# The last block's queries, keys, convolution input and gates: from TensorE transposes to VectorE blocks and a trip through DRAM

## The reference, cut to what matters

```
def hybrid_mixer(h, w_in, b_merge, conv_w, w_out_conv, w_out_attn, w_o):
    B, S, _ = h.shape
    proj = jnp.einsum("bsd,dc->bsc", h, w_in)
    splits = np.cumsum([D_CONV] * 4 + [D_ATTN] * 4 + [D_MODEL])
    xc, bg, cg, zc, q, k, v, za, g_conv, g_attn = jnp.split(proj, splits, axis=-1)

    c = causal_depthwise_conv(cg * xc, conv_w)
    y_conv = jnp.einsum("bsc,cd->bsd", jax.nn.silu(zc) * bg * c, w_out_conv)

    shp = (B, S, N_HEADS, HEAD_DIM)
    o = mixture_of_dilations(q.reshape(shp), k.reshape(shp), v.reshape(shp),
                             alibi_slopes(N_HEADS)).reshape(B, S, D_ATTN)
    y_attn = jnp.einsum("bsc,cd->bsd", jax.nn.silu(za) * o, w_out_attn)
    ...
    merged = g_conv * y_conv + g_attn * y_attn
    return jnp.einsum("bsd,de->bse", merged, w_o)
```

## Time and profile before

| | us |
|---|---|
| median of 3 runs | 1367.21 |
| lowest, highest | 1365.07, 1367.71 |
| the profiled execution, its own time | 1366.17 |
| its span in the profile | 1364.4 |
| PE busy, of the span | 1348.8 |
| VectorE, ScalarE, GpSimd busy | 624.0, 658.0, 1140.3 |

### The profile page before, as it was taken

One profiled execution on the slowest core, in us unless ns is written; L12 is line 12 of the kernel. 1 busy time (PEld: TensorE's weight loads), 2 busy tenths in 40 slices (PEclk: granted clock), 3 DMA queues, 4 the chain that ended last, 5 costly groups with the idle time before them and its releaser, 6 DMA issues.

```text
span 1364.4 us, 19630 instructions
## 1 busy us (share of the span) xinstructions
PE 1348.8 (99%) x6723; PEld 1121.2 (82%) x6723; DVE 624.0 (46%) x1570; ACT 658.0 (48%) x757; POOL 1140.3 (84%) x913
## 2 busy tenths in 40 slices
PE   8999999999999999999999999999999999999997
PEld 6888888888888888888888778888888888878886
DVE  6233344654333356623333885333346236862224
ACT  6444454546444456444443676444446443444431
POOL 5999977849999969999998539999978977779882
PEclk9999999999999999999999999999999999999999
DMA  8666654536666555766558426665545557767540
GB/s 273 215 201 208 206 183 144 185 106 225 197 192 194 194 171 171 237 210 211 184 184 217 139 77 208 210 198 187 184 154 196 192 193 202 215 183 256 190 165 31
DMA packets 199488, 255.36 MB, mean 187 GB/s; under 512 B 42844, under 2 KB 137860, under 8 KB 199300
## 3 DMA queue, kind: packets, MB, share of 16 engines
q1 hardware_dynamic: 197140, 247.82, 57.0%
q10 hardware_dynamic: 2288, 6.75, 1.4%
HBM read 249.29 MB, written 5.24 MB: 187 GB/s over the span
## 4 chain that ended last, share of the span: by engine, by line
PE 92%; DVE 4%; ACT 1%; DMA 1%; issue 1%; SPq 0%; ACTq 0%; DVEq 0%
PE tb L2152 9%; PE gu L2152 9%; PE acc L2062 8%; PE acc L2063 8%; PE acc L2065 7%; PE acc L2099 6%; PE acc L2102 6%; PE acc L2107 6%; PE gu L2062 5%; PE gu L2063 5%; PE tb L2158 4%; PE gu L2158 4%; PE gu L2065 3%; PE gu L2070 2%; PE tb L2065 1%; PE tb L2062 1%
## 5 line engine op out<-in xcount | busy, mean ns | idle before, releaser
L642 POOL TENSOR_TENSOR w_lo<-w_raw,w_hi 128x512 fp32r<-128x512 f32 x896 | 1135.3, 1315 | 197.1 <-ACT w_hi L675 193.7
L675 ACT CAST w_hi<-w_raw 128x2048 fp32r<-128x2048 f32 x225 | 427.8, 1909 | 146.1 <-DMA w_raw<-in_w_ffn_in 36.3
L2152 PE MATMUL gu<-xT,w_hi 128*128 128x512 f32 x512 | 202.3, 395 | 0.0
L2152 PE MATMUL tb<-xT,w_hi 128*128 128x512 f32 x512 | 202.2, 395 | 0.0
L2062 PE MATMUL acc<-w_hi,xT 128*128 128x512 f32 x496 | 198.3, 400 | 0.0
L2063 PE MATMUL acc<-w_lo,xT 128*128 128x512 f32 x496 | 193.1, 389 | 0.0
L2065 PE MATMUL acc<-w_hi,xT 128*128 128x512 f32 x468 | 182.7, 390 | 0.0
L1378 DVE TENSOR_TENSOR arena<-gu,arena 128x256 f32<-128x256 f32 x64 | 27.2, 425 | 300.5 <-PE gu L2152 300.5
L2158 PE MATMUL tb<-xT,w_lo 128*128 128x256 f32 x512 | 140.4, 280 | 0.0
L2158 PE MATMUL gu<-xT,w_lo 128*128 128x256 f32 x512 | 139.8, 279 | 0.0
L2062 PE MATMUL gu<-w_hi,xT 128*128 128x512 f32 x312 | 123.4, 395 | 1.1 <-ACT xT L720 1.1
(11 more groups left out here) (364 smaller groups left out, 1969.0 us busy)
## 6 DMA issues: line engine op xcount, KB each, us to landing
w_raw<-in_w_ffn_in SPq DMA_DIRECT2D x176, 512.0 KB, 4.7
w_raw<-in_w_ffn_out SPq DMA_DIRECT2D x88, 512.0 KB, 4.1
w_raw<-in_w_in SPq DMA_DIRECT2D x80, 512.0 KB, 4.6
w_raw<-in_mlstm_w_in SPq DMA_DIRECT2D x24, 512.0 KB, 4.3
w_raw<-in_w_ple_gate SPq DMA_DIRECT2D x16, 512.0 KB, 4.1
w_raw<-in_w_kv SPq DMA_DIRECT2D x16, 512.0 KB, 4.3
w_raw<-in_mlstm_w_out SPq DMA_DIRECT2D x8, 512.0 KB, 4.5
w_raw<-in_diff_w_q SPq DMA_DIRECT2D x8, 512.0 KB, 5.2
```

The costliest lines, as they stand in the source:

```text
L642: ins = pool.tensor_tensor(w_lo[:, slot.spl, cols], w_raw[:, slot.raw, cols], w_hi[:, slot.spl, cols].bitcast(F32), ALU.subtract)
L675: nc.scalar.copy(w_hi[:, slot.spl, :], w_raw[:, slot.raw, :]).then_inc(hi_ready, 1)
L2152: return mm(pair_of(j), w_hi[:, slot.spl, at:at + P], xT[:, 4 * half + k, :, :].rearrange("p a c -> p (a c)"), start=(half == 0 and k == 0 ...
```

## The change

The eight units leave PE, ACT and the PSUM buffer `tb`. In their place DVE turns each tile of a unit in 32x32 blocks (`turn_unit`, one 128x512 transpose a tile, right behind `take`), SP stores the 128x1024 blocks of a unit into a DRAM buffer of its own in four DMAs, one for 32 partitions each (`scatter_blocks`, `store_unit`), and one DMA of 128 rows of 4096 bytes loads them to their places (`load_unit`). `H_STORE_UNITS` and `H_LOAD_UNITS` name the slots of HI behind whose load SP does this.

The stores now place the blocks: a piece is 32 floats, 128 bytes, a DMA of a unit has 1024 of them, and one of a heads' trip 768. The load is contiguous in DRAM. Before, a heads' trip stored 128 pieces of 768 bytes in each DMA and loaded in pieces of 128 bytes. Its store and load are now apart (`store_heads`, `load_heads`), the load one slot later, and `h_pb` has two buffers, the second in the constants' tables. DVE's transposes read with a step of four elements. The convolution moves a group later, and the convolution's gates are multiplied as 128x1024 from SBUF (`gate_conv`). `b_merge` is loaded in two halves, the second once the gates are used.

```diff
-H_CONVOLVE = {(9, 0): 0, (9, 1): 1, (10, 0): 2, (10, 1): 3, (11, 0): 4, (12, 0): 5, (12, 1): 6, (13, 0): 7}
-
-H_UNITS_AT = {(2, 0): 0, (2, 1): 1, (3, 0): 2, (4, 0): 3, (8, 1): 7, (10, 1): 9, (12, 1): 11, (14, 1): 13}
+H_CONVOLVE = {(10, 0): 0, (10, 1): 1, (11, 0): 2, (11, 1): 3, (13, 0): 4, (13, 1): 5, (14, 0): 6, (14, 1): 7}
+
+H_GATE_AT = {(15, 0): 11, (17, 0): 13}
+
+H_UNITS = (0, 1, 2, 3, 7, 9, 11, 13)
+H_BLOCKS_FREE = {7: 3, 9: 7, 11: 0, 13: 11}
+
+H_STORE_UNITS = {10: (0, 1), 12: (2,), 14: (3,), 22: (7,), 27: (9,), 31: (11,), 34: (13,)}
+H_LOAD_UNITS = {11: (0, 1), 13: (2,), 15: (3,), 23: (7,), 28: (9,), 32: (11,), 35: (13,)}
...
 
                 sp.wait_ge(h_blocks_turned, 2 * m + 2)
-                if m:
-                    sp.wait_ge(h_pt_landed, 64 * m)
-                for i in range(4):
-                    sp.dma_start(h_bounce[m % 2][i].rearrange("(j b) n -> b j n", j=4), h_pb[32 * i:32 * i + 32]
-                                 ).then_inc(h_bounced, 16)
+                scatter_blocks(h_bounce[m % 2], h_pb[m % 2], h_bounced)
+
+            def load_heads(m):
+
                 if m >= 2:
                     sp.wait_ge(h_pv_in_psum, 2 * m - 2)
+                if m:
+                    sp.wait_ge(h_pt_landed, 16 * m)
                 sp.wait_ge(h_bounced, 64 * (m + 1))
-                for i in range(4):
-                    sp.dma_start(h_pT[:, m % 2, :, 32 * i:32 * i + 32],
-                                 h_bounce[m % 2][i].rearrange("c (n a) -> c n a", a=32)).then_inc(h_pt_landed, 16)
-
-            def linear(s0, w, cols, halves_first=False, after={}):
+                sp.dma_start(h_pT[:, m % 2].rearrange("p n c -> p (n c)"), h_bounce[m % 2]).then_inc(h_pt_landed, 16)
+
+            def store_unit(c):
+
+                sp.wait_ge(h_unit_turned, H_UNIT_NO[c] + 2)
+                scatter_blocks(h_unit_bounce[c], h_blocks[c], h_unit_stored)
+
+            def load_unit(c):
+
+                n = H_UNITS.index(c)
+                sp.wait_ge(h_unit_stored, 128 if n < 2 else 64 * (n + 1))
+                if n:
+                    sp.wait_ge(h_unit_landed, 16 * n)
+                sp.dma_start(h_turned[c].rearrange("p k c -> p (k c)"), h_unit_bounce[c]).then_inc(h_unit_landed, 16)
...
+            def turns_after(i):
+
+                m = i - H_TURN_SLOT
+                if m >= 0 and m % 2 == 0 and m // 2 < AH // 2:
+                    store_heads(m // 2)
+                if m >= 1 and m % 2 == 1 and m // 2 < AH // 2 - 1:
+                    load_heads(m // 2)
+                if m == AH - 2:
+                    load_heads(AH // 2 - 1)
+                for c in H_LOAD_UNITS.get(i, ()):
+                    load_unit(c)
+                for c in H_STORE_UNITS.get(i, ()):
+                    store_unit(c)
...
-                def units(c):
-
-                    dst = H_UNITS[c]
-                    for t in range(TILES):
-                        w = H_UNIT_NO[c] + t
-                        act.wait_ge(h_pl_in_psum, w + 1)
-                        nc.scalar.copy(dst[:, :, tok(t)], tb[:, 1, :].rearrange("p (k c) -> p k c", k=4)
-                                       ).then_inc(h_pl_ready, 1)
...
-                        if H_UNITS.get(H_UNITS_AT.get((c, j))) is not None:
-                            units(H_UNITS_AT[c, j])
...
-                        act.dma_start(h_bm, A["b_merge_2"].broadcast_to([P, 2 * D])).then_inc(h_bm_landed, 16)
+                        act.dma_start(h_bm[:, D:2 * D], A["b_merge_2"][:, 0:D].broadcast_to([P, D])
+                                      ).then_inc(h_bm_landed, 16)
...
+                act.wait_ge(h_z_ready, 4)
+                act.wait_ge(h_bm_landed, 16)
+                act.dma_start(h_bm[:, 0:D], A["b_merge_2"][:, D:2 * D].broadcast_to([P, D])).then_inc(h_bm_landed, 16)
...
-                        if h >= 2 and h % 2 == 0:
-                            dve.wait_ge(h_bounced, 64 * (h // 2))
-                        to = h_pb[:, :, 96 * (h % 2):96 * (h % 2) + 96].rearrange("p j (n a) -> p n j a", n=3)
-                        v.transpose(to, s.rearrange("p (n j b) -> p n j b", n=3, j=4)).then_inc(h_blocks_turned, 1)
+                        if h >= 4 and h % 2 == 0:
+                            dve.wait_ge(h_bounced, 64 * (h // 2 - 1))
+                        to = h_pb[(h // 2) % 2][:, :, 96 * (h % 2):96 * (h % 2) + 96].rearrange("p j (n a) -> p n j a", n=3)
+                        v.transpose(to, s.rearrange("p (n b j) -> p n j b", n=3, j=4)).then_inc(h_blocks_turned, 1)
...
+                def turn_unit(c):
+
+                    if c in H_BLOCKS_FREE:
+                        dve.wait_ge(h_unit_stored, 64 * (H_UNITS.index(H_BLOCKS_FREE[c]) + 1))
+                    for t in range(TILES):
+                        dve.wait_ge(h_evac, H_EVAC[c] - 1 + t)
+                        to = h_blocks[c].rearrange("p j (k t a) -> p t k j a", t=TILES, a=32)[:, t]
+                        v.transpose(to, h_s[:, H_PLACE[c], t, :].rearrange("p (k b j) -> p k j b", j=4, b=32)
+                                    ).then_inc(h_unit_turned, 1)
...
+                    if c in H_UNITS:
+                        turn_unit(c)
...
-                    dve.wait_ge(h_pl_ready, 10 + 2 * (k // 4))
+                    dve.wait_ge(h_unit_landed, 16 * (5 + k // 4))
...
-                def z_units(c):
+                def gate_conv(c):
 
                     half = (c - 11) // 2
                     dve.wait_ge(h_conv, 4 * half + 4)
-                    for t in range(TILES):
-                        dve.wait_ge(h_pl_in_psum, H_UNIT_NO[c] + t + 1)
-                        z = h_zT[:, 4 * half:4 * half + 4, tok(t)]
-                        v.tensor_tensor(z, tb[:, 1, :].rearrange("p (k c) -> p k c", k=4), z, ALU.mult
-                                        ).then_inc(h_z_ready, 1)
+                    dve.wait_ge(h_unit_landed, 16 * (H_UNITS.index(c) + 1))
+                    z = h_zT[:, 4 * half:4 * half + 4, :]
+                    v.tensor_tensor(z, h_turned[c], z, ALU.mult).then_inc(h_z_ready, 2)
...
-                            pe.wait_ge(h_pl_ready, 8)
+                            pe.wait_ge(h_unit_landed, 48)
+                        elif h == 8:
+                            pe.wait_ge(h_unit_landed, 64)
...
-                        pe.wait_ge(h_pt_landed, 64 * (h // 2 + 1))
+                        pe.wait_ge(h_pt_landed, 16 * (h // 2 + 1))
...
-                def unit(c, t):
-                    pe.wait_ge(h_evac, H_EVAC[c])
-                    w = H_UNIT_NO[c] + t
-
-                    if 0 < w <= 12:
-                        pe.wait_ge(h_pl_ready, w)
-                    elif w > 12:
-                        pe.wait_ge(h_z_ready, w - 12)
-                    for k in range(4):
-                        ins = nc.tensor.transpose(tb[:, 1, tok(k)], h_s[:, H_PLACE[c], t, tok(k)], ident[:])
-                    ins.then_inc(h_pl_in_psum, 1)
...
-                            if (c, j) in H_UNITS_AT:
-                                unit(H_UNITS_AT[c, j], t)
```

81 lines of the change are left out of this document (46 added, 35 removed).

## The result

| | before | after |
|---|---|---|
| median of the runs made side by side, us | 1366.81 (22 runs) | 1368.95 (22 runs) |
| lowest, highest | 1365.07, 1368.63 | 1366.5, 1372.53 |
| profiled execution, its span | 1366.17, 1364.4 | 1367.35, 1365.6 |

The changed kernel takes 1.0015 of the time before, with a 95% interval of 1.0009 to 1.0021: no change that matters, and 10 us above the forecast. The spread of the runs also grew, from 3.6 to 6 us.

The account below looks back on a forecast made before the run. PE was taken to bound the kernel. Transposes (7.1 us) and waits (1.5) leaving PE sum to 8.6 us, with nothing charged against them: 1367.2 - 8.6 = 1358.6 us; forecast 1356.5 to 1360.5 (chance 0.60), range 1356 to 1366.

Parts of the forecast that it names:

- 2 us to spare in trip 0 and 3 to 6 later: Heads' trips in HI: their loads land before PE's product needs them, by 2 us in trip 0, 3 to 6 later.
- 8.6 us leave PE: PE in HI: 16 groups of unit transposes, 7.1 us, and two waits that leave with them, 1.5 us.
- Written 128-byte pieces at 13 ns: Stores into DRAM: a 128-byte piece takes 13 ns, as in loads; no row had this price, 48 kept as upper bound.
- The rivals at 26 and 48 ns: Stores into DRAM: written pieces cost 26 ns, 1365.5 us, chance 0.08; or near 48 ns, 1382.4 us, chance 0.14 (slower).
- Step 0 at 1101.7: Start of HI's scores: PE comes to step 0 at 1101.7, eight transpose groups earlier than 1105.26.
- 3.1 us are left: Step 0, by a walk through SP's queue with before's times: unit 2's load lands at 1098.6, 3.1 us before PE.
- Transposes at 0.70 us: VectorE: 16 unit transposes of 128x512 at 0.70 us, 11 us in all, nothing for the step; bounds 0.70 and 1.4.
- Issuing a store takes 0.74 us: SP's queue: issuing a unit's store of 1024 pieces takes about 0.74 us, four 3.0.
- The weights lose 6 of their 16 us of lead and win them back: Weight loads ahead of step 0: 6 of 16 us lead lost, regained as GpSimd takes 5.0 us a slot, PE 5.4.
- The rival of VectorE as the bound: VectorE at c = 11 becomes the bound: 1 to 3 us, 1360 to 1362; chance counted within small waits' 0.18.
- The 7.1 us at slot 39 stay: End of HI: the weights' lead over PE at slot 39 stays 7.1 us.
- the first, small waits: Rival: step 0 or a trip comes late, costing PE 1 to 4 us at one or two places; 1360.5 to 1364.5, chance 0.18.

Follow-up runs that it names:

- experiment 3: Changed kernel with the four early units stored and loaded one at a time, order 0, 2, 1, 3, step 0 waiting for two: 1362.7 us, ratio 0.9972.
- the version without waits: Changed kernel with early units one at a time in order 0, 2, 1, 3 and trip 6's load ahead of slot 32's weight load: 1358.78 us, ratio 0.9938.
- experiments 4, 6, 7 and 8: Changed kernel with trip 0 earlier (1368.38 us); old-form trips (1366.97); GpSimd pausing at HC's start (1369.54); trip 6's load ahead of slot 32's weights (1366.71).
- experiment 8: Changed kernel with trip 6's load ahead of slot 32's weight load: 1366.71 us, ratio 0.9996; with early units also one at a time: 1358.78 us.

## Why the prediction was wrong, point by point

The gain in the sum held. What failed is what the sum put at nothing: the wait of the heads' trips, "2 us to spare in trip 0 and 3 to 6 later". In the profiled run trip 0 cost 4.6 us and 2.0 more at the lower clock, trip 6 cost 3.1, a third product 0.2, together 9.9.

- **8.6 us leave PE: right.** The span of experiment 3 follows from it within 0.2 us, and the version without waits runs at 1358.78, where the forecast was 1358.6. So close a match is in part luck: the profiled runs of these kernels come to step 0 up to 2.4 us apart.
- **Written 128-byte pieces at 13 ns: right.** Over 1040:1115 the median of such a store's packet was 13 ns. The rivals at 26 and 48 ns fall, and with them a second pass as a price that shows in a packet's time.
- **Step 0 at 1101.7: right** (1101.67). **"3.1 us are left": wrong, nothing was.** Unit 2 landed at 1101.64, where the walk had 1098.6. The walk's 1085 for slot 12's load was 1086.44, and unit 2's stores behind it took 6.06 us to issue instead of 3.0. That PE hardly waited there in this run was luck; with other kernels of the same early part it waited 0.2 to 0.9 us (experiments 4, 6, 7 and 8).
- **Transposes at 0.70 us: wrong, the term was 1.09.** The bounds, 0.70 and 1.4, held it; the heads' transposes went unpriced, though the same step reads them (0.86 for 0.57). Together this is 16 x 0.39 + 16 x 0.30 = 11 us more. It is not what made the most of VectorE's lateness at step 14 (1.1 of 5.7 us); the part of the convolution that moved there, 4.2 us, was priced nowhere.
- **Issuing a store takes 0.74 us: wrong where stores follow one another behind weights.** Four take 4.6 to 7.3 us. The walk priced the packets and the issue apart, and let SP run ahead of the engines without a bound. Experiment 3 keeps these long issues and keeps the lead too, so this error alone did not cost the time.
- **"The weights lose 6 of their 16 us of lead and win them back": this step failed.** The lead over PE was 12.8 us at slot 10, not 16, and 7.7 at slot 15. The loss of some 6 us was well sized (5.1), but two things around it were not. The 16 us were before's, measured to a PE that comes 3.6 us later; the prediction took these 3.6 us off for step 0 and not for the lead. And "win them back" has its own price in the prediction: at 5.4 - 5.0 = 0.4 us a slot, 6 us take 15 slots, and trip 0 depends on slot 16. The walk ended at step 0, with the most visible deadline. The one after it, trip 0, has its stores in SP's queue behind slot 19's load, which waits for slot 16's low part. "2 us to spare in trip 0" had been counted with before's times for that load.
- **Trips with 3 to 6 us to spare later: wrong for trip 6,** by a chain that the prediction had parts of: VectorE late at c = 11, ScalarE's exponentials, its rounding of slot 29, slot 32's load, and the trip's load behind it. The rival of VectorE as the bound was priced at PE's wait for maxima; the wait came by way of SP's queue instead. That the load's place is needed for the wait is shown (experiment 8); how much of VectorE's lateness comes from the convolution's new place is read from one trace, and no run moved it back.
- **The 7.1 us at slot 39 stay: wrong without harm,** 3.9 are left.
- **A lower clock was in no term.** Behind the longer wait it took 2 us more.

The rival that came true was the first, small waits, in kind; its size (1 to 4 us) was too small, since the two waits came in one run and the clock fell with the longer. Its place, step 0 or a trip, was named.

## What to carry to other kernels

A DMA that is issued in order with weight loads has two deadlines: its own, and that of everything behind the load that stands ahead of it; walk a lost lead forward to the next transfer that waits for a weight's place in the queue, not only to the first consumer. And measure a lead against the engine as it will run after the change: one that gets less to do arrives earlier and uses up lead by itself. When a gain on the bound engine vanishes, list that engine's waits before doubting the gain: here another order of the units and one load moved past another brought 10 us back. And change the step of an operand's reading only with its price in hand, on every instruction that gets it.
